# Four buffer slots of split weights at byte offsets of 0, 8, 16 and 48

## What is computed

```python
x = x + 0.5 * swiglu(rms_norm(x, norm_ffn1_w), gate1, up1, down1)    # 2048 -> 5632 -> 2048
x = x + head_group_mixer(rms_norm(x, norm_mix_w), w_in, ..., w_out)  # 2048 -> 5376 ... -> 2048
x = x + 0.5 * swiglu(rms_norm(x, norm_ffn2_w), gate2, up2, down2)
return rms_norm(x, norm_final_w)

def swiglu(h, w_gate, w_up, w_down):
    return (silu(h @ w_gate) * (h @ w_up)) @ w_down
```

## Time and profile before

| | |
|---|---|
| Time, median of 3 runs | 1844.76 us (1844.43 to 1845.06) |
| The profiled execution: its time | 1844.38 us |
| its span, first to last instruction | 1842.6 us |
| TensorE matmuls (PE) | 1830.3 us busy, 8570 instructions |
| TensorE weight loads (PEld) | 1537.5 us |
| VectorE (DVE) | 1045.0 us |
| ScalarE (ACT) | 832.0 us |
| GpSimd (POOL) | 63.3 us |
| DMA | 346.61 MB, mean 188 GB/s |

### The profile page before, as it was taken

The page is one execution under the profiler, slowest core; times in us unless marked ns, Lnnn a source line. Parts: engine busy times, 40 slices in busy tenths (PEclk is TensorE's granted clock), DMA queues, the critical chain, the costliest instruction groups (busy, mean ns, idle before and its releaser), DMA issues.

```text
span 1842.6 us, 23062 instructions
## 1 busy us (share of the span) xinstructions
PE 1830.3 (99%) x8570; PEld 1537.5 (83%) x8570; DVE 1045.0 (57%) x1087; ACT 832.0 (45%) x996; POOL 63.3 (3%) x59
## 2 busy tenths in 40 slices
PE   9999999999999999999999999999999999999998
PEld 7888888888888888999998888888888888888886
DVE  5565465455556557555557665555555556546546
ACT  7444443444444444555555455444444444444344
POOL 0000000000000000000009000000000000000000
PEclk9999999999999999999999999999999999999999
DMA  9565555555555555555555456555556565565552
GB/s 367 195 194 186 193 190 186 197 185 191 195 183 187 200 183 172 179 179 167 172 160 180 137 182 206 183 190 197 183 192 193 184 195 190 187 195 188 190 198 92
DMA packets 177345, 346.61 MB, mean 188 GB/s; under 512 B 6048, under 2 KB 31008, under 8 KB 177184
## 3 DMA queue, kind: packets, MB, share of 16 engines
q1 hardware_dynamic: 176880, 345.61, 57.0%
q10 hardware_dynamic: 432, 0.55, 0.1%
HBM read 344.04 MB, written 2.10 MB: 188 GB/s over the span
## 4 chain that ended last, share of the span: by engine, by line
PE 98%; DMA 0%; DVE 0%; issue 0%; ACT 0%; SPq 0%; POOLq 0%; POOL 0%; DVEq 0%
PE ps L325 32%; PE ps L327 32%; PE ps L326 32%; PE ps L352 2%; DMA raw<-in_g 0%; PE ps L477 0%; PE ps L561 0%; PE ps L572 0%; PE ps L490 0%; PE ps L446 0%; PE ps L445 0%; PE ps L444 0%; DVE x L895 0%; DVE proj L1082 0%; DVE w_lo L846 0%
## 5 line engine op out<-in xcount | busy, mean ns | idle before, releaser
L846 DVE TENSOR_TENSOR w_lo<-raw,w_hi 128x1024 fp32r<-128x1024 f32 x656 | 812.9, 1241 | 770.6 <-ACT w_hi L636 770.0
L636 ACT ACTIVATE w_hi<-raw 128x1024 fp32r<-128x1024 f32 x656 | 695.0, 1061 | 979.9 <-PE ps L327 969.7
L325 PE MATMUL ps<-w_hi,xT_hi 128*128 128x512 f32 (+1 forms) x1848 | 714.6, 387 | 0.9 <-DVE xT_lo L859 0.9
L327 PE MATMUL ps<-w_hi,xT_lo 128*128 128x512 f32 (+1 forms) x1848 | 710.1, 384 | 0.0
L326 PE MATMUL ps<-w_lo,xT_hi 128*128 128x512 f32 (+1 forms) x1848 | 709.9, 384 | 0.0
L325 PEld LDWEIGHTS ps<-w_hi,xT_hi 128*128 128x128 f32 x1848 | 347.1, 188 | 63.7 <-DVE xT_lo L859 1.3
L327 PEld LDWEIGHTS ps<-w_hi,xT_lo 128*128 128x128 f32 x1848 | 347.0, 188 | 63.0
L326 PEld LDWEIGHTS ps<-w_lo,xT_hi 128*128 128x128 f32 x1848 | 347.2, 188 | 61.6
L325 PE MATMUL ps<-w_hi,hT_hi 128*128 128x512 f32 x640 | 249.1, 389 | 0.0
L327 PE MATMUL ps<-w_hi,hT_lo 128*128 128x512 f32 x640 | 249.0, 389 | 0.0
L326 PE MATMUL ps<-w_lo,hT_hi 128*128 128x512 f32 x640 | 249.0, 389 | 0.0
(11 more groups left out here) (109 smaller groups left out, 514.0 us busy)
## 6 DMA issues: line engine op xcount, KB each, us to landing
raw<-in_u SPq DMA_DIRECT2D x88, 1024.0 KB, 5.1
raw<-in_d SPq DMA_DIRECT2D x88, 1024.0 KB, 4.9
raw<-in_g SPq DMA_DIRECT2D x87, 1024.0 KB, 5.1
raw<-in_w_in SPq DMA_DIRECT2D x48, 896.0 KB, 4.6
raw<-in_w_out SPq DMA_DIRECT2D x16, 1024.0 KB, 4.9
x<-in_x SPq DMA_DIRECT2D x4, 512.0 KB, 12.7
out<-proj SPq DMA_DIRECT2D x8, 256.0 KB, 2.4
proj<-in_xT SPq DMA_DIRECT2D x3, 512.0 KB, 9.8
```

Source lines behind the costliest of these rows:

```text
L325: pe.matmul(out, xh, wh, start=first and j == 0, stop=False)
L327: mm = pe.matmul(out, xl, wh, start=False, stop=last and j == 1)
L636: act.activation(dst, raw[:, s, (k % 2) * HALF:(k % 2 + 1) * HALF], ACT.Copy).then_inc(hi_ready, 1)
L846: dve.tensor_tensor(w_lo[:, k % LEAD, :, :].rearrange(flat), raw[:, k // 2, (k % 2) * HALF:(k % 2 + 1) * HALF], f32(w_hi[:, k % LEAD, :, : ...
```

## The change

The slots' starts within w_hi and w_lo get an extra offset of 0, 2, 4 and 12 elements, so 0, 8, 16 and 48 bytes (SLOT_SHIFT). Both tensors become flat, with 64 elements (256 bytes) more at the end, so that w_lo starts 256 bytes further in SBUF and everything behind it 512. A new function `slot` gives the 1024 elements of a slot, and `part` the 512 (or 448) columns of one of its two tiles. All places that used w_hi and w_lo go through these two; the instructions, their sizes, their order and their waits stay.

```diff
--- before.py
+++ after.py
@@ -43,6 +43,8 @@
 RAW = 4
 LEAD = 4
 HALF = 2 * W
+SLOT_SHIFT = (0, 2, 4, 12)
+SLOT_PAD = 64
 
 
 G_FFN = [0, 3 * NF + NI + 4]
@@ -110,8 +112,8 @@
         xT_hi = sb("xT_hi", [P, KT, SEQ], F32R)
         xT_lo = sb("xT_lo", [P, KT, SEQ], F32R)
         raw = sb("raw", [P, RAW, 4 * W])
-        w_hi = sb("w_hi", [P, LEAD, 2, W], F32R)
-        w_lo = sb("w_lo", [P, LEAD, 2, W], F32R)
+        w_hi = sb("w_hi", [P, LEAD * HALF + SLOT_PAD], F32R)
+        w_lo = sb("w_lo", [P, LEAD * HALF + SLOT_PAD], F32R)
         proj = sb("proj", [P, T, D_IN])
         cos = sb("cos", [P, T, RD // 2])
         sin = sb("sin", [P, T, RD // 2])
@@ -234,6 +236,13 @@
 
             return (0, 1, 2, 3, 4, 5, 2, 3)[p]
 
+        def slot(w, k):
+            c0 = k % LEAD * HALF + SLOT_SHIFT[k % LEAD]
+            return w[:, c0:c0 + HALF]
+
+        def part(w, k, j, width=W):
+            return slot(w, k)[:, j * W:j * W + width]
+
         def f32(ap):
             return ap.bitcast(F32)
 
@@ -321,7 +330,7 @@
                     for t in range(T):
                         out = ps[:, bank + t, 0:width]
                         xh, xl = (a[:, kt + j, t * P:(t + 1) * P] for a in (a_hi, a_lo))
-                        wh, wl = (w[:, k % LEAD, j, 0:width] for w in (w_hi, w_lo))
+                        wh, wl = (part(w, k, j, width) for w in (w_hi, w_lo))
                         pe.matmul(out, xh, wh, start=first and j == 0, stop=False)
                         pe.matmul(out, xh, wl, start=False, stop=False)
                         mm = pe.matmul(out, xl, wh, start=False, stop=last and j == 1)
@@ -334,17 +343,17 @@
                 outs = [ps[:, B_GATE + t, :] for t in range(T)]
                 for j in range(2):
                     for t in range(T):
-                        pe.matmul(outs[t], xT_hi[:, 2 * k + j, t * P:(t + 1) * P], w_hi[:, k % LEAD, j, :],
+                        pe.matmul(outs[t], xT_hi[:, 2 * k + j, t * P:(t + 1) * P], part(w_hi, k, j),
                                   start=k == 0 and j == 0, stop=False)
                 pe.wait_ge(lo_ready, k + 1)
                 for j in range(2):
                     for t in range(T):
-                        pe.matmul(outs[t], xT_hi[:, 2 * k + j, t * P:(t + 1) * P], w_lo[:, k % LEAD, j, :],
+                        pe.matmul(outs[t], xT_hi[:, 2 * k + j, t * P:(t + 1) * P], part(w_lo, k, j),
                                   start=False, stop=False)
                 pe.wait_ge(xT_lo_ready, k + 1)
                 for j in range(2):
                     for t in range(T):
-                        mm = pe.matmul(outs[t], xT_lo[:, 2 * k + j, t * P:(t + 1) * P], w_hi[:, k % LEAD, j, :],
+                        mm = pe.matmul(outs[t], xT_lo[:, 2 * k + j, t * P:(t + 1) * P], part(w_hi, k, j),
                                        start=False, stop=False)
                 mm.then_inc(half_used, 1)
 
@@ -439,7 +448,7 @@
                             if t == 0 and kt % 2 == 0:
                                 pe.wait_ge(lo_ready, 8 * g + 2 * n + kt // 2 + 1)
                             out = ps[:, B_DOWN + 2 * (n % 2) + t, :]
-                            wh, wl = (w[:, (2 * n + kt // 2) % LEAD, kt % 2, :] for w in (w_hi, w_lo))
+                            wh, wl = (part(w, 2 * n + kt // 2, kt % 2) for w in (w_hi, w_lo))
                             xh, xl = (a[:, kt, t * P:(t + 1) * P] for a in (last_hT_hi, last_hT_lo))
                             pe.matmul(out, xh, wh, start=kt == 0, stop=False)
                             pe.matmul(out, xh, wl, start=False, stop=False)
@@ -632,8 +641,7 @@
                     act.wait_ge(first_half_loaded, 16)
                 elif k % 2 == 0 or (first and k == 1):
                     act.wait_ge(raw_loaded[s], 16 * g + 16)
-                dst = w_hi[:, k % LEAD, :, :].rearrange("p k c -> p (k c)")
-                act.activation(dst, raw[:, s, (k % 2) * HALF:(k % 2 + 1) * HALF], ACT.Copy).then_inc(hi_ready, 1)
+                act.activation(slot(w_hi, k), raw[:, s, (k % 2) * HALF:(k % 2 + 1) * HALF], ACT.Copy).then_inc(hi_ready, 1)
 
             def position(g, k):
                 if not (isinstance(g, int) and 8 * g + k + LEAD >= HALVES):
@@ -842,10 +850,9 @@
 
                 g, k = g + k // 8, k % 8
                 dve.wait_ge(hi_ready, 8 * g + (k + 1))
-                flat = "p k c -> p (k c)"
-                dve.tensor_tensor(w_lo[:, k % LEAD, :, :].rearrange(flat),
+                dve.tensor_tensor(slot(w_lo, k),
                                   raw[:, k // 2, (k % 2) * HALF:(k % 2 + 1) * HALF],
-                                  f32(w_hi[:, k % LEAD, :, :].rearrange(flat)), ALU.subtract).then_inc(lo_ready, 1)
+                                  f32(slot(w_hi, k)), ALU.subtract).then_inc(lo_ready, 1)
 
             def position(g, k):
                 if not (isinstance(g, int) and 8 * g + k + LEAD >= HALVES):
```

## The result

The changed kernel takes 1880.65 us (median of 4 runs, 1880.59 to 1880.81), the kernel before in the same comparison 1844.81 us (4 runs): a ratio of 1.0195, interval 1.0177 to 1.0212. It is 35.8 us slower. The profiled execution took 1880.61 us, with a span of 1878.8 us, 36.2 more than before.

A forecast was written before the change was run, and what follows sets the result against it. TensorE was taken as the bound, matmul count times beat. The profiled 1844.38 us plus 27.5 for lost beats, other terms 0, gave 1871.9; with the median 0.4 higher and 1 us off for existing run-ins, 1871 us, range 1812 to 1887.

The forecast's parts named there:

- What bounds the kernel: TensorE, busy 99% of the 1842.6 us span: time is the number of matmuls times the distance between two starts.
- Step (a): TensorE's moving reads in the shifted slots: 4734 matmuls of three slots lose 5.8 ns each, +27.5 us.
- settled state: Aligned, undisturbed 512-column xT matmuls start every 226.7 ns, the shortest seen for this type.
- attT's beat: Matmuls with attT, 128 bytes off alignment, start every 232.5 ns; 5.8 ns more was taken as the loss.
- The second road of the same step: A run-in in each of 656 halves, 10 of 12 beats at +4.3 ns: +22.6 us; if short, +7 us.
- What of w_lo's 256 bytes: Slot 0 keeps its offset, but its w_lo reads, 256 bytes further, do not quite; no separate size given.
- Step (b): The 1152 matmuls of 448 columns, taken as already outside the good state: 0, bounds -5 and +5 us.
- Steps (c) and (d): ScalarE and VectorE on shifted slots, covered up to 2720 ns per half; buffers behind w_lo moved 512 bytes: both 0.
- The faster rival: Offsets take the two TensorE reads apart and win back part of 13.4 ns per beat: 1789 to 1840 us, chance 0.36.
- No effect: Rival: offsets this small leave TensorE's reads as they are, 1845 to 1848 us, chance 0.14.
- one read more per line: Columns read in small groups, a start within one costing one read more per matmul: +2.7 us for a slot.
- The rule that I set against the forecast: Skill's issue gap, N / 2.4 + 2.5 ns, 215.8 ns at 512 columns: no address matters, time stays at 1845.

The follow-up runs named there:

- line_32: The kernel before with everything from x on 32 bytes further, all distances between tensors kept: 1845.14 us, ratio 1.0002.
- pad_only: The changed kernel with its pads but all four slot offsets 0: 1844.72 us, ratio 1.0000 against the kernel before.
- frame_zero: Kernel before with w_lo 512 bytes further, four small tensors moved from ahead of x to behind w_hi, all slot offsets 0: 1844.62 us, ratio 1.0001.
- all_16: The changed kernel with one offset of 16 bytes for all four slots: 1873.81 us, ratio 1.0159 against the kernel before.
- step_64: The changed kernel with slot offsets of 0, 64, 128 and 192 bytes: 1871.40 us, ratio 1.0146 against the kernel before.
- all_32: The changed kernel with one offset of 32 bytes for all four slots: 1888.30 us, ratio 1.0237 against the kernel before.

## Why the prediction was right

The forecast was slower, 1871 us in a range of 1812 to 1887, and 1880.65 was measured. The range held both signs, and slower had a chance of 0.50, so the sign was half a matter of luck; the mechanism behind it is the one that the runs show.

*What bounds the kernel*, the time as a number of matmuls times the beat, held: 6312 x 5.7 ns is the whole difference.

*Step (a)*, slower through the loss of the settled state, was right in its mechanism and its sign. Its size was off: it priced three slots of four with attT's beat and got 27.5 us; measured are 35.8, next to the upper end it gave, all 6312 matmuls, 36.6. So this term was too small by a quarter. What was missing is slot 0. The second road of the same step had it, a run-in at each entry into a slot, but I set it beside the first as another way to the same sum, where it adds to it: slots 1 to 3 have unsettled beats of their own (235, 232, 233 ns), and slot 0 has its ten beats of run-in. A quarter of 6312 x (230 - 226.7) is another 5 us, and slots 1 and 3 are above attT's 232.5. That the run-in has ten beats was taken from the earlier trace rows alone, where the breaks behind transposes of `h` have two; that it came out as ten was partly luck. The step speaks of slots that leave the alignment, and does not say whether their own start counts or its distance to the stationary operand; the runs show that it is the distance, and that a common shift of both costs nothing (line_32).

*What of w_lo's 256 bytes* was left half open there ("its w_lo reads do not quite") and is nothing: pad_only.

*Step (b)*, priced at 0, came out at 256.26 and 256.64 us, but not for its reason. It took the 448-column matmuls to be outside the good state already and so untouched; away from breaks and slot changes included, the trace has 205.2 ns in slot 1 and 202.3 in slot 2 where the kernel before has 202.9, and over the four slots this cancels to 0.4 us.

*Steps (c) and (d)*, priced at 0, were right: 1240 and 1062 ns for the splits with VectorE and ScalarE still waiting for work, and frame_zero and pad_only for the moved buffers.

*The faster rival* was wrong here and in every offset tried, for 512 columns: 13.4 ns per beat are still spent on something, and no distance tried has a mean below 226.6. For 448 columns one distance, 16 bytes, was faster by 2 us in all_16. *No effect* was wrong, also in the form of one read more per line. The rule that I set against the forecast, of the Trainium skill, TensorE: Matmul & The Clock Gate, section Back-to-back issue gap (215.8 ns at 512 columns, there called the gap of a single isolated matmul), knows no addresses; the runs show 226.7 to 236.7 ns for the same matmul at the same clock, by address alone.

*Not settled.* That the moving read meets the read of the next stationary tile, and loses time where they meet, is argued from the distance between the two; no run here took the weight loads away, or showed a collision. The weight loads themselves last 187.8 ns on average before and 188.4 after. That the distance counts within 256 bytes rests on 256 and 512 being as good as 0 (pad_only, frame_zero). Distances between those of the table were not tried. What makes a run-in two beats long or ten is not known. And why -16 bytes is worse than all others is open.

## What to carry to other kernels

Where TensorE is the bound with fp32r operands, read the beat from the starts of the timeline, not from the busy time, and compare it across stationary tensors: two values for the same shape can be an address at work, and moving one tensor shows it. For 512 columns keep the moving and the stationary operand at the same offset within 256 bytes; a common shift of 32 bytes did no harm. Do not give the buffers of a ring offsets of their own: in this kernel that keeps 36 us. A jump of the distance costs the slot with the good distance as well: its first ten matmuls of 12 are unsettled in the changed kernel, at 40 ns per entry (20 in step_64). Other shapes have to be measured: with 448 columns 16 bytes were slightly better than 0.

## What was not expected of the hardware

The unsettled beats are not noise. In the changed kernel's stretch four halves take 76.85 - 65.69 = 11.16 us, and the next four 88.01 - 76.85 = 11.16 us again: a mean of 232 ns is a pattern that repeats. One matmul form had means from 226.7 ns to 236.7 ns, at a granted clock of 0.998 or 0.999 over each run. A shift of all tensors by 32 bytes left the time within 0.3 us (line_32); a shift of the moving ones alone by as much cost 43.5 us (all_32).
